# Decoder trunk on one core: the compressed value product stacked in its contraction, and another order of the first transfers and products

## What is computed

```python
k_cmp = compress(kc, pe[0], w1[0], w2[0])
v_cmp = compress(vc, pe[1], w1[1], w2[1])        # 15 compressed blocks
s_c = jnp.einsum('btghd,bcgd->bghtc', qg, k_cmp) * scale
p_c = masked_softmax(s_c, c_end[None, :] <= t[:, None])
o_cmp = jnp.einsum('bghtc,bcgd->btghd', p_c, v_cmp)
...
o = gates[..., 0:1] * o_cmp + gates[..., 1:2] * o_sel + gates[..., 2:3] * o_win
```

## Time and profile before

| | |
|---|---|
| time, median of 3 runs | 2225.67 us (2225.6 to 2226.52) |
| the profiled execution, its own time | 2226.44 us |
| span of its first to last instruction | 2224.3 us |
| mean granted TensorE clock | 0.999 |
| busy: PE, DVE, ACT | 2213.0, 1596.7, 1154.4 us |

### The profile page before, as it was taken

How to read it: one execution, slowest core, us unless ns; L and a number is a source line. 1 busy time by engine, 2 the same in 40 slices (tenths; PEclk the granted TensorE clock), 3 DMA queues, 4 the chain that set the end, 5 groups by cost and what they waited for, 6 DMA issues and landing times.

```text
span 2224.3 us, 26335 instructions
## 1 busy us (share of the span) xinstructions
PE 2213.0 (99%) x10106; PEld 1836.9 (83%) x10106; DVE 1596.7 (72%) x2202; ACT 1154.4 (52%) x1590; POOL 18.7 (1%) x20
## 2 busy tenths in 40 slices
PE   9999999999999999999999999999999999999998
PEld 7888888888888888888888888888888888888887
DVE  7777675788878888544566678757987888884444
ACT  7556674655454544444574545556545454544443
POOL 0000000000000000000030000000000000000000
PEclk9999999999999999999999999999999999999999
DMA  8554556667776777676655853457776777766664
GB/s 321 192 169 155 186 174 194 210 235 222 239 234 221 227 231 235 198 227 199 196 170 183 267 158 96 138 166 222 238 239 226 228 226 234 239 215 202 192 194 153
DMA packets 128284, 458.99 MB, mean 206 GB/s; under 512 B 14784, under 2 KB 17088, under 8 KB 127392
## 3 DMA queue, kind: packets, MB, share of 16 engines
q1 hardware_dynamic: 127888, 456.78, 64.3%
q0 software_dynamic: 128, 0.49, 0.1%
q10 hardware_dynamic: 144, 0.05, 0.0%
HBM read 443.72 MB, written 2.10 MB: 200 GB/s over the span
## 4 chain that ended last, share of the span: by engine, by line
PE 99%; DVE 0%; DMA 0%; ACT 0%; SPq 0%; issue 0%; DVEq 0%; ACTq 0%
PE bank L612 98%; PE bank L764 0%; PE bank L778 0%; DMA raw<-in_mem 0%; PE bank L805 0%; DVE lo L1279 0%; PE bank L901 0%; PE bank L908 0%; DVE x L1432 0%; PE bank L754 0%; PE bank L902 0%; PE bank L906 0%; PE bank L905 0%; PE bank L903 0%; ACT h L1036 0%; DVE h L1327 0%
## 5 line engine op out<-in xcount | busy, mean ns | idle before, releaser
L1279 DVE TENSOR_TENSOR lo<-raw,hi 128x1024 fp32r<-128x1024 f32 x775 | 945.0, 1224 | 504.8 <-ACT hi L984 498.6
L612 PE MATMUL bank<-hi,h 128*128 128x512 f32 x3904 | 1227.2, 392 | 1.2 <-ACT h L1036 1.0
L984 ACT ACTIVATE hi<-raw 128x1024 fp32r<-128x1024 f32 x775 | 817.0, 1060 | 778.7 <-PE bank L612 747.9
L612 PEld LDWEIGHTS bank<-hi,h 128*128 128x128 f32 x3904 | 732.8, 188 | 154.0 <-ACT h L1036 1.5
L612 PE MATMUL bank<-lo,h 128*128 128x512 f32 x1952 | 759.9, 389 | 0.0
L612 PE MATMUL bank<-hi,mid 128*128 128x512 f32 x1408 | 433.7, 389 | 0.0
L612 PEld LDWEIGHTS bank<-lo,h 128*128 128x128 f32 x1952 | 366.7, 188 | 73.9
L612 PEld LDWEIGHTS bank<-hi,mid 128*128 128x128 f32 x1408 | 264.3, 188 | 54.7
L612 PE MATMUL bank<-lo,mid 128*128 128x512 f32 x704 | 273.9, 389 | 0.0
L612 PE MATMUL bank<-hi,o 128*128 128x512 f32 x512 | 164.5, 394 | 0.0
L1530 DVE STREAM_TRANSPOSE cv<-mf 32x256 f32<-32x256 f32 x352 | 153.4, 436 | 6.5
(11 more groups left out here) (244 smaller groups left out, 1183.2 us busy)
## 6 DMA issues: line engine op xcount, KB each, us to landing
raw<-in_gate SPq DMA_DIRECT2D x176, 512.0 KB, 4.1
raw<-in_up SPq DMA_DIRECT2D x176, 512.0 KB, 3.7
raw<-in_down SPq DMA_DIRECT2D x176, 512.0 KB, 4.2
raw<-in_in SPq DMA_DIRECT2D x136, 512.0 KB, 4.1
raw<-in_out SPq DMA_DIRECT2D x64, 512.0 KB, 3.6
taps<-in_taps SPq DMA_DIRECT2D x44, 512.0 KB, 5.2
raw<-in_mem SPq DMA_DIRECT2D x31, 512.0 KB, 4.5
st<-st SPq DMA_DIRECT2D x22, 448.0 KB
```

The costliest lines, as they stand in the source:

```text
L612: return mm(out, lhsT, rhs, start=first, stop=last, skip_group_check=True)
L984: act(hi[k][:, 0:w], raw[k][:, 0:w], ACT.Copy).then_inc(hi_done, 1)
L1279: tt(lo[k][:, 0:w], raw[k][:, 0:w], hi[k][:, 0:w].bitcast(F32), ALU.subtract).then_inc(lo_done, 1)
```

## The change

- **Compressed product** (`hidT`, `cmp`, `nsaS`, `nsaB`, `nsaC`): the 15 weights of a token are written four times into one `psc` of 128 columns, for both halves of the tokens; one transpose replaces two; ScalarE rounds the transposed tile to fp32r (`pct`), VectorE replaces its upper 64 rows by the rest; the value side holds the rounded values and their rest in matching rows (`vcmp[t]`, made once). One fp32r product of 128 columns per token half then sums all terms over its contraction.
- **Beginning** (`first_wide`, `second_piece`): pieces 0 and 1 are loaded, rounded and split in halves, and TensorE waits term by term; tiles 0 and 1 of the memory are asked for by ScalarE's queue; the idle products are 4 1/2 instead of 5; the splitting of tiles 2 and 3 (`feed_mem` 0, 1) comes one tick earlier, ahead of piece 2's.

```diff
 # SP
                 if n == 0:
                     sp_.dma_start(raw[0][:, 0:W], kv_piece(c, p)[:, 0:W]).then_inc(s_first, 16)
-                    sp_.dma_start(memT[:, 0:1, :], A["memT"][:, 0:1, :]).then_inc(s_first_mem, 16)
                     sp_.dma_start(raw[0][:, W:2 * W], kv_piece(c, p)[:, W:2 * W]).then_inc(landed[0], 16)
-                    sp_.dma_start(memT[:, 1:2, :], A["memT"][:, 1:2, :]).then_inc(s_second_mem, 16)
+                    return
+                if n == 1:
+                    sp_.dma_start(raw[1][:, 0:W], kv_piece(c, p)[:, 0:W]).then_inc(s_second, 16)
+                    sp_.dma_start(raw[1][:, W:2 * W], kv_piece(c, p)[:, W:2 * W]).then_inc(landed[1], 16)
                     return
 # TensorE
+            def first_wide(c, n):
+                take_banks(c)
+                for q in range(2):
...
+                    pe_.wait_ge(*((hi_done, n + 1) if q else (first_whi, n + 1)))
+                    pe_.wait_ge(*((mhi_done, 1) if q else (first_mhi, 1)))
+                    for t in range(2):
+                        add(out[t], amem[:, q, 0, half(t)], w_hi, q == 0, False)
+                    pe_.wait_ge(*((lo_done, n + 1) if q else (first_wlo, n + 1)))
+                    for t in range(2):
+                        add(out[t], amem[:, q, 0, half(t)], w_lo, False, False)
+                    pe_.wait_ge(*((mlo_done, 1) if q else (first_mlo, 1)))
+                    for t in range(2):
+                        m = add(out[t], amem[:, q, 1, half(t)], w_hi, False, False)
+                m.then_inc(piece_done, 1)
...
-                            m = add(B[b][0:NC, g * P:(g + 1) * P], hs[:, 1, c, g * NC:(g + 1) * NC], w2[:, 1, c, :],
+                            m = add(B[b][:, g * P:(g + 1) * P], hsd[:, c, g, :], w2[:, 1, c, :],
                                     g == 0 and c == 0)
...
-                take(6, npt_act, hd + 1)
+                take(6, npt_dve, 2 * hd + 2)
...
-                for t in range(2):
-                    tr(B[6][:, T + t * P:T + (t + 1) * P], psc[:, t, :], ident)
+                tr(B[6][:, T:T + P], psc[:, :], ident)
...
-                pe_.wait_ge(npt_act, hd + 1)
-                pe_.wait_ge(npt_dve, hd + 1)
+                pe_.wait_ge(npt_act, 2 * hd + 1)
+                pe_.wait_ge(npt_dve, 2 * hd + 2)
...
-                add(O[:, 0:T], vcmp[:, g, :], pts[:, T:2 * T], False, False)
+                for t in range(2):
+                    add(O[:, half(t)], vcmp[t][:, g, :], pct[:, :], False, False)
 # ScalarE
             act_.dma_start(gains[:], A["gains"]).then_inc(s_gains, 16)
+            act_.dma_start(memT[:, 0:1, :], A["memT"][:, 0:1, :]).then_inc(s_first_mem, 16)
+            act_.dma_start(memT[:, 1:2, :], A["memT"][:, 1:2, :]).then_inc(s_second_mem, 16)
...
-                act(pts[:], B[6][:, :], ACT.Copy).then_inc(npt_act, 1)
+                act(pts[:], B[6][:, 0:T], ACT.Copy).then_inc(npt_act, 1)
+                act(pct[:], B[6][:, T:T + P], ACT.Copy).then_inc(npt_act, 1)
 # VectorE, cmp(1): once
-                    copy(vcmp[0:NC].rearrange("p g d -> p (g d)"), B[7][0:NC, 0:T]).then_inc(cmp_done, 1)
+                    finish(copy(vh[:], B[7][:, 0:T]))
+                    for t in range(2):
+                        v, at = vcmp[t][:].rearrange("p g d -> p (g d)"), C_PICK + 2 * t
+                        finish(ts(ve[:], B[7][:, 0:T], cst[:, at:at + 1], None, ALU.mult))
+                        m = stt(v, vh[:].bitcast(F32), cst[:, at + 1:at + 2], ve[:], ALU.mult, ALU.add)
+                        if t == 0:
+                            finish(m)
+                    m.then_inc(cmp_done, 1)
 # VectorE, nsaS
-                parts = [psc[:, 0, 0:NC], psc[:, 1, 0:NC], ps0[:, 0, :], ps0[:, 1, :], ps1[:, 0, :], ps1[:, 1, :]]
+                for t in range(2):
+                    ts(psc[:].rearrange("p (b t m) -> p b t m", b=2, t=2)[:, :, t, 0:2 * NC].rearrange("p b (r n) -> p b r n", r=2),
+                       pc[t].rearrange("p (b r n) -> p b r n", b=1, r=1).broadcast_to((P, 2, 2, NC)), wgt[:, t:t + 1], None, ALU.mult)
+                parts = [ps0[:, 0, :], ps0[:, 1, :], ps1[:, 0, :], ps1[:, 1, :]]
 # VectorE, nsaB
                 copy(ptw[:], B[7][:, :]).then_inc(npt_dve, 1)
+                dve.wait_ge(npt_act, 2 * hd + 2)
+                low = pct[0:P // 2, :]
+                tt(low, B[6][0:P // 2, T:T + P], low.bitcast(F32), ALU.subtract).then_inc(npt_dve, 1)
```

More of the change, by code:

```diff
@@ L403, in build @@
         shadow = [("o_b", [P, DT, 2, T], F32R), ("memT_b", [P, DT, T], F32)] + [(n + "_b", s, d) for n, s, d in common]
-        (v1, cosf, sinf, ropeD, w2, pe, ps0, ps1, psc, pts, ptw, G) = region(
+        (v1, cosf, sinf, ropeD, w2, pe, ps0, ps1, psc, pts, ptw, G, vcmp1, pct, pcr) = region(
             shadow + [("v1", [P, 2, W], F32), ("cosf", [P, 2, P], F32), ("sinf", [P, 2, P], F32),
@@ L407, in build @@
                       ("pe", [P, 2, CMP_LEN], F32), ("ps0", [P, 2, P], F32), ("ps1", [P, 2, T], F32),
-                      ("psc", [P, 2, P], F32), ("pts", [P, W], F32), ("ptw", [P, W], F32),
-                      ("G", [P, HEADS, 6], F32)])[len(shadow):]
+                      ("psc", [P, P], F32), ("pts", [P, T], F32), ("ptw", [P, W], F32),
+                      ("G", [P, HEADS, 6], F32), ("vcmp1", [P, GROUPS, P], F32R), ("pct", [P, P], F32R),
+                      ("pcr", [P, 2, NC + 1], F32)])[len(shadow):]
         row2, = region(shadow + [("v1_c", [P, 2, W], F32), ("row2", [P, D], F32)])[len(shadow) + 1:]
@@ L415, in build @@
         blk, blkf = [blk0, blk1], [blkf0, blkf1]
+        vcmp, pc = [vcmp0, vcmp1], [pcr[:, t, 0:NC] for t in range(2)]
         quarters = [[memT[:, 4 * q:4 * q + 4, :] for q in range(4)], [m[:] for m in (mem_a, mem_b, mem_c, mem_d)]]
@@ L630, in wide @@
                 kt0 = c.kts[p]
[L631 to L634, removed]
+                if c.gate and c.gate[0] == "m":
                     pe_.wait_ge(mlo_done, 8 * c.gate[1] + p + 1)
@@ L931, in _ @@
             pe_.wait_ge(idle_set, 1)
-            for _ in range(5):
+            for _ in range(4):
                 add(B[7][:, 0:T], st[:, 0, 0, 0:P], st[:, 0, 0, 0:T], True)
+            add(B[7][:, 0:P], st[:, 0, 0, 0:P], st[:, 0, 0, 0:P], True)
             for n, (c, p) in enumerate(PLAN.pieces):
-                if n:
+                if n > 1:
                     pe_.wait_ge(lo_done, n + 1)
-                if n in APART:
+                if n < 2:
+                    first_wide(c, n)
+                elif n in APART:
                     apart(c, p, n)
@@ L970, in first_pieces, with second_piece @@
                 act(amem[:, 1, 0, :], memT[:, 1, :], ACT.Copy, scale=gains[:, 0, 2, 1:2]).then_inc(mhi_done, 1)
+            def second_piece():
+                act_.wait_ge(s_second, 16)
+                act(hi[1][:, 0:W], raw[1][:, 0:W], ACT.Copy).then_inc(first_whi, 1)
+                act_.wait_ge(landed[1], 16)
+                act(hi[1][:, W:2 * W], raw[1][:, W:2 * W], ACT.Copy).then_inc(hi_done, 1)
             def round_piece(n):
@@ L1265, in first_pieces, with second_piece @@
                 memory_rest(1).then_inc(mlo_done, 1)
+            def second_piece():
+                dve.wait_ge(first_whi, 2)
+                tt(lo[1][:, 0:W], raw[1][:, 0:W], hi[1][:, 0:W].bitcast(F32), ALU.subtract).then_inc(first_wlo, 1)
+                dve.wait_ge(hi_done, 2)
+                tt(lo[1][:, W:2 * W], raw[1][:, W:2 * W], hi[1][:, W:2 * W].bitcast(F32), ALU.subtract).then_inc(lo_done, 1)
             def split_piece(n):
@@ L1697 @@
             consts[:, C_PAR + 2 * t + j] = np.arange(P) % 2 == j
+    rows, slot = np.arange(P) // 32 % 2, np.arange(P) % 32 // NC
+    for t in range(2):
+        consts[:, C_PICK + 2 * t] = (rows == t) & (slot == 1)
+        consts[:, C_PICK + 2 * t + 1] = (rows == t) * np.select([slot == 0, slot == 1], [1.0, -1.0])
     consts[:, C_EPS] = EPS
```

48 lines of the change are left out of this document (30 added, 18 removed).

## The result

The changed kernel takes 2243.06 us (median of 6 runs, 2242.83 to 2245.02) where the kernel before takes 2226.09 (6 runs on the same chip): a ratio of 1.0078, 95% interval 1.0065 to 1.0091. The forecast was 2223.6 with a range of 2221.3 to 2225.4. The span is 2241.0 us at a mean granted clock of 0.999, so it isn't the clock, the only rival that the prediction had for a slower kernel.

A forecast was written before the change was run, and what follows sets the result against it. TensorE, busy 99% of the span, was taken as the bound. Gains of 0.8 (beginning), 0.1 (product with w2) and 1.1 (heads), 2.0 us, took 2225.67 to 2223.7, rounded to 2223.6; range 2221.3 to 2225.4.

The forecast's parts named there:

- the clock: Rival: TensorE's clock stays at the lower level through pieces 0 to 3, giving 2232.5 us; chance 0.03.
- the sum: Whole kernel: gains of 0.8 (beginning), 0.1 (product with w2) and 1.1 (heads) make 2.0 us.
- a piece of 12 takes 2.71: TensorE's price in us for a piece of 12 products of 512 columns, 0.2256 each, from the old chain.
- The beginning: First pieces: TensorE starts earlier until piece 2's data binds; gain 0.8 us, bounds 0 and 2.3.
- The heads on TensorE: NSA heads: one transpose less each and a cheaper compressed product save 0.32 us a head, 3.8 if TensorE never waits.
- The product with w2: Second compressed product: it loses its shape of 15 columns; gain 0.1 us, bounds 0 and 0.2.
- What the heads give back: NSA heads: VectorE's additions, 0.28 us a head, make TensorE's value products wait; 2.7 of 3.8 us come back.

The follow-up runs named there:

- e1: Changed kernel with filler `line` cut from 84 to 80 columns, so amem, o and mid lie at their old place: 2222.75 us.
- e6: Changed kernel with `line` at 112 columns, so amem, o and mid lie 128 bytes behind their old place: 2239.35 us.
- e9: Kernel before with x and h 32 bytes earlier, hi, lo, amem, o and mid staying: 2260.23 us.
- e10: Changed kernel with `line` at 144 columns, so amem, o and mid lie 256 bytes behind their old place: 2222.73 us.
- e7: Kernel before with only the beginning of the change; constants, `line` and NSA heads as before: 2224.59 us.
- e12: e1 with memory tiles 0 and 1 asked for by SP again instead of ScalarE: 2223.41 us.
- e2: Kernel before with `line` grown from 88 to 96 columns, so everything behind it lies 32 bytes further: 2246.5 us.
- e4: Kernel before with h, raw, hi and lo 32 bytes further, amem, o and mid at their old place: 2246.11 us.
- e3: Changed kernel with `line` at 96 columns, so amem, o and mid lie 64 bytes behind their old place: 2242.75 us.
- e5: Kernel before with stationary operands, pieces and everything behind them all 32 bytes further: 2226.34 us.

## Why the prediction was wrong

- **The failed step is the sum, which has no term for where tiles lie.** It costs everything that an engine executes and takes for granted that "a piece of 12 takes 2.71" also after the change. 272 pieces take 0.08 more: 20.3 us, ten times the forecast's 2.0 and against it. What a piece costs depends on the distance in SBUF between its stationary and its moving operand (e1 to e6, e9, e10). With the tiles back in place the changed kernel takes 2222.75 (e1), inside the range and 0.9 below the forecast. "Slower by over 0.2% is the clock alone: 0.03" was therefore wrong in its reason as much as in its size. The rows of before could not give the price, but the diff gave the occasion: 4 columns more in `cst`, 4 less in a filler in front of the largest region, which only makes sense if a place is being held.
- **The beginning: right mechanism, mis-sized.** 0.8 us was forecast; the medians give 1.7 (e7), before's trace and e1's 1.76, inside the bounds of 0 and 2.3. Piece 2's data is what binds in e1, as said, but it came 0.89 us earlier than the one trace that the forecast read, which was late by 0.5 against four others of the same beginning. The prediction took from the Trainium skill ("Trainium Kernel Development and Optimization", Key Constraints) that a second queue saves only issue time, and made of it that the two moved requests give nothing. But issue time is what they save: SP issues piece 2's request 0.95 us earlier in e1 than in e12, and the median is 0.66 us shorter. So the runs agree with the sentence, and the step from it to nothing was wrong.
- **The heads on TensorE: right.** A head's value products to the next piece, before and in e1:

```profile
1344.87 0.59 PE L612 MATMUL bank<-pts,v 128*128 128x256 f32 x2
...
1346.52 0.47 PE L612 MATMUL bank<-hi,h 128*128 128x512 f32 x1
```

```profile
1363.89 0.59 PE L618 MATMUL bank<-pts,v 128*128 128x256 f32 x2
1364.13 0.52 PE L618 MATMUL bank<-pct,vcmp 128*128 128x128 f32 x2
1364.49 1.09 PE L618 MATMUL bank<-ptw,v 128*128 128x256 f32 x6
1365.33 0.48 PE L618 MATMUL bank<-hi,h 128*128 128x512 f32 x1
...
1373.39 0.59 PE L618 MATMUL bank<-pts,v 128*128 128x256 f32 x2
```

  1.65 us before, 1.44 in e1: the forecast 0.21, though the distances inside are other ones (`pct` 0.36, not 0.22, but the pair ahead of it 0.24 instead of 0.43). Without `rope` the period is 9.50 instead of 9.82 (1365.63 to 1375.45 before): the forecast 0.32.
- **The product with w2: mis-sized.** From the last product ahead of it to the first piece behind it and a memory head 2.08 us before (1289.24 to 1291.32), 1.81 in e1 (1287.46 to 1289.27): 0.27, where 0.1 and at most 0.2 was forecast.
- **What the heads give back: right place, a little too dear.** The waits came in heads 1, 2, 5 and 6, and the distance from `ptw` to the maxima is 0.80. But VectorE's two multiplications cost 0.05 more and not 0.08 (1344.76 to 1345.09 in e1 against 0.28):

```profile
1344.76 0.41 DVE L1670 TENSOR_SCALAR psc<-pcr,wgt 128x60 f32<-128x60 f32 x2
1345.09 1.00 DVE L1674 TENSOR_SCALAR ps<-ps,wgt 128x128 f32<-128x128 f32 x4
```

  With the product with w2 done, e1 leads by 1291.32 - 1289.27 = 2.05 us; at head 2's value product by 1354.81 - 1353.38 = 1.43. Of the 0.75 saved by then nothing is left and 0.62 more is lost, 1.37 in all (forecast 1.5). In heads 4 to 6 the lead falls from 2.06 to 1.63, so 1.07 is given back (forecast 1.2). Of 3.8 us 2.4 come back and not 2.7.
- **Together** 1.76 + 0.27 + 3.8 - 2.44 = 3.4 us, the lead over before's trace that e1's has in the last stretch (3.40); the medians say 3.3. So without the place of the tiles the kernel gains 3.3 us where 2.0 was forecast: the right side, and mis-sized in the beginning above all.

## What to carry to other kernels

Before you believe that an edit leaves the rest of a kernel alone, compare the addresses of its large operands before and after, with the rounding of every tile; here a constant that grew by 16 bytes cost 20.3 us, six times the 3.3 that the edit wins. If unbroken stretches of the same instructions change their length in the trace, as here by 7.06 us, look past waits and past the work edited: group the instructions by operand, and look for what the slow groups share. Where an engine's unbroken chain sets another's waits, an operation that nobody ahead needs belongs behind the one they wait for; here that could not be told from leaving it out (2222.03 and 2221.92).

## What the runs showed of the hardware

- For a product of 128 x 128 with 512 columns in fp32r, the distance in SBUF between stationary and moving operand counts, not the place of either. At the old distances, which are multiples of 256 bytes, and at 256 more, products start 0.2267 us apart (2.72 / 12); at 32 bytes to either side (e2, e4, e9) or 64 more (e3) 0.2333 (2.80 / 12, 3% more), at 128 more (e6) 0.2325 (2.79 / 12). Moving both by 32 bytes costs nothing (e5). In the last pieces of before and after, where all other engines and the DMA are at rest, it is the same. Other distances, types and shapes were not tried, and why it is so, no view shows.
- The modelled durations of such products show it faintly (389 or 392 ns against 395 or 397); the distances of starts and the length of long stretches show it plainly.
- In e1 two fp32r products of 128 columns with a stationary operand each stand 0.36 us ahead of what follows, and the pair of instructions of a plain fp32 product of 256 columns takes 0.24 where they follow it; before, 0.43 where another plain fp32 product does. Only the sum of a group should be forecast from such rows.
